# Modulation sums on TensorE, an input projection begun with the first half of them, and low parts made by VectorE

## What is computed

```python
mod = silu(c) @ w_ada + b_ada                       # c: (1, 2048), w_ada: (2048, 6 x 2048)
sh1, sc1, gt1, sh2, sc2, gt2 = split(mod, 6)
h = rms_norm(x, g_norm1) * (1 + sc1) + sh1
proj = h @ w_in                                     # 2048 x 3904: q, k, v (differential), latents cq, ckv, k_pe
a_out = differential_attention(...)                 # 8 heads
b_out = latent_attention(... w_q_b, w_kv_b ...)     # 8 heads
x = x + gt1 * (concat(a_out, b_out) @ w_out)
h2 = rms_norm(x, g_norm2) * (1 + sc2) + sh2
x = x + gt2 * ((silu(h2 @ w_gate) * (h2 @ w_up)) @ w_down)   # width 5632
```

## Time and profile before

| | |
|---|---|
| runs | 2667.58, 2671.43, 2675.92 us |
| profiled execution, span from first to last instruction | 2674.8 us |
| PE / PEld busy | 87% / 71% of the span |
| DVE / ACT / POOL busy | 40% / 37% / 78% |
| DMA, mean | 193 GB/s, 516.02 MB |

### The profile page before, as it was taken

The page is one execution under the profiler, slowest core; times in us unless marked ns, Lnnn a source line. Parts: engine busy times, 40 slices in busy tenths (PEclk is TensorE's granted clock), DMA queues, the critical chain, the costliest instruction groups (busy, mean ns, idle before and its releaser), DMA issues.

```text
span 2674.8 us, 29475 instructions
## 1 busy us (share of the span) xinstructions
PE 2319.1 (87%) x10218; PEld 1890.4 (71%) x10218; DVE 1066.6 (40%) x1189; ACT 1000.3 (37%) x1189; POOL 2095.1 (78%) x862
## 2 busy tenths in 40 slices
PE   0168984788899999999997966899999999999987
PEld 0157763476788888888886845787888888888765
DVE  4676458878611222111118399513111111111244
ACT  0023333433444444444443322344444444444433
POOL 0078965698888888888886875798888888888886
PEclk9879996789899999999998988999999999999998
DMA  7877744557666666666664633356666666666543
GB/s 254 261 258 246 253 158 137 185 189 266 236 200 206 207 205 205 205 205 208 205 204 142 190 117 102 126 190 191 190 189 190 192 189 189 190 192 189 173 151 133
DMA packets 241636, 516.02 MB, mean 193 GB/s; under 512 B 16429, under 2 KB 22274, under 8 KB 238882
## 3 DMA queue, kind: packets, MB, share of 16 engines
q1 hardware_dynamic: 239168, 512.55, 60.2%
q10 hardware_dynamic: 2402, 2.60, 0.6%
HBM read 510.90 MB, written 4.19 MB: 193 GB/s over the span
## 4 chain that ended last, share of the span: by engine, by line
PE 63%; DVE 8%; issue 3%; POOL 3%; DMA 3%; ACT 1%; DVEq 0%; SPq 0%; ACTq 0%
PE ps L1755 60%; DMA ada_raw<-in_w_ada 3%; POOL w_lo L816 2%; DVE ada_acc L1245 1%; DVE conv L928 1%; PE ps L1672 1%; POOL fm_lo L833 1%; PE ps L1770 1%; PE ps L1723 0%; DVE rstd L1177 0%; DVE y L1143 0%; DVE conv L1009 0%; PE ps L1897 0%; DVE x L1545 0%; DVE z L1267 0%
## 5 line engine op out<-in xcount | busy, mean ns | idle before, releaser
L816 POOL TENSOR_TENSOR w_lo<-raw,w_hi 128x1024 fp32r<-128x1024 f32 (+1 forms) x766 | 1921.9, 2517 | 464.7 <-ACT w_hi L574 464.0
L574 ACT ACTIVATE w_hi<-raw 128x1024 fp32r<-128x1024 f32 (+1 forms) x766 | 808.9, 1057 | 1389.1 <-PE ps L1755 1291.4
L1755 PE MATMUL ps<-w_hi,fm_hi 128*128 128x512 f32 (+1 forms) x2176 | 861.8, 396 | 83.5 <-POOL w_lo L816 59.9
L1755 PE MATMUL ps<-w_hi,fm_lo 128*128 128x512 f32 (+1 forms) x2176 | 851.9, 392 | 0.0
L1755 PE MATMUL ps<-w_lo,fm_hi 128*128 128x512 f32 (+1 forms) x2176 | 851.5, 391 | 0.0
L1755 PEld LDWEIGHTS ps<-w_hi,fm_hi 128*128 128x128 f32 x2176 | 413.2, 190 | 189.2 <-POOL w_lo L816 58.9
L1755 PEld LDWEIGHTS ps<-w_lo,fm_hi 128*128 128x128 f32 x2176 | 412.9, 190 | 86.7
L1755 PEld LDWEIGHTS ps<-w_hi,fm_lo 128*128 128x128 f32 x2176 | 413.5, 190 | 82.6
L1755 PE MATMUL ps<-w_hi,hid_hi 128*128 128x512 f32 x704 | 277.3, 394 | 2.5 <-issue 2.5
L1755 PE MATMUL ps<-w_lo,hid_hi 128*128 128x512 f32 x704 | 275.1, 391 | 0.0
L1755 PE MATMUL ps<-w_hi,hid_lo 128*128 128x512 f32 x704 | 274.9, 391 | 0.0
(11 more groups left out here) (281 smaller groups left out, 1801.0 us busy)
## 6 DMA issues: line engine op xcount, KB each, us to landing
raw<-in_w_gate SPq DMA_DIRECT2D x176, 512.0 KB, 3.7
raw<-in_w_up SPq DMA_DIRECT2D x176, 512.0 KB, 3.7
raw<-in_w_down SPq DMA_DIRECT2D x176, 512.0 KB, 3.7
ada_raw<-in_w_ada SPq DMA_DIRECT2D x160, 512.0 KB, 5.0
raw<-in_w_in SPq DMA_DIRECT2D x120, 512.0 KB, 3.7
raw<-in_w_out SPq DMA_DIRECT2D x64, 512.0 KB, 3.9
ada_wide<-in_w_ada SPq DMA_DIRECT2D x16, 1024.0 KB, 5.7
raw<-in_w_ple_gate SPq DMA_DIRECT2D x32, 512.0 KB, 3.7
```

The lines of the kernel that those rows point to most:

```text
L574: act.activation(w_hi[:, hi_slot, :, 0:width], raw[:, slot, :, 0:width], ACT.Copy).then_inc(hi_ready, 1)
L816: pool.tensor_tensor(w_lo[:, slot, :, 0:width], raw[:, slot, :, 0:width], w_hi[:, hi_slot, :, 0:width], ALU.subtract).then_inc(lo_ready, 1)
L1755: last = pe.matmul(banks[t][:, 0:width], a, b, start=kt == 0 and k == 0, stop=kt == kts - 1 and k == 2)
```

## The change

- w_ada for the first five vectors comes in 80 pieces of 128 rows by 2048 columns (1 MB) in five groups of 16: first half of sh1 and sc1, second half, the same of sh2 and sc2, then gt1. TensorE takes a piece as four fp32 matmuls of 32 columns of weights (c_act repeated 32 times) by 512 columns, each into its own 32 partitions of one PSUM bank (`ada`). A finished group is copied by ScalarE (`copy_rows`), turned by four transposes (`turn_columns`) and read by VectorE (`modulation`); for gt1 four matmuls spread the rows (`spread_gate`).
- The operand is turned and copied to `fm_t` before the modulation is known. in1 begins with the first half of the k-tiles of its first three units (pieces 0 to 11), with group 1's pieces between them; the second half follows. Groups 2 and 3 lie in in1 and q_b, group 4 in attention, one piece a step.
- VectorE makes the low parts of pieces 0 to 105 (`rest`), and the low parts of the operands up to out1 (`h1_lo`, `turned_lo`); GpSimd starts with the feed-forward.
- b_ada for gt1 is loaded after attention. `ada_acc` is only for gt2. A few PSUM banks change places.

```diff
-RAW, SPLIT, ADA = 6, 3, 4
+RAW, SPLIT = 6, 3
+ADA = 4
+ADA_GROUPS = ((0, 2, 0), (0, 2, 1), (3, 5, 0), (3, 5, 1), (2, 3, None))
+LO_DVE = FIRST["ffn1"]
+IN1_ORDER = (6, 7, 0, 1, 2, 3, 4, 5)
+IN1_HALVES = 3
@@ SyncE
+            def ada(n):
+                if n >= ADA:
+                    sp.wait_ge(ada_used, n - ADA + 1)
+                first, end, half = ADA_GROUPS[n // KT]
...
+            for n in range(10):
+                ada(n)
+            for n in range(RAW):
+                ada(10 + n)
+                weights(n)
+            for n in range(16, 22):
+                ada(n)
+            for i in range(12):
+                weights(i + RAW)
+                ada(22 + i)
+            for n in range(34, 38):
+                ada(n)
+            for i in range(12, FIRST["out1"]):
+                weights(i + RAW)
+                if i < FIRST["q_b"] and i % 4 == 3:
+                    ada(38 + (i - 15) // 2)
+                    ada(39 + (i - 15) // 2)
...
+            sp.wait_ge(ada_used, ADA_PIECES)
+            sp.dma_start(gate[:, :], ...)
@@ VectorE
+            def rest(p):
+                slot, width = p % RAW, in1_width(p) if p < FIRST["q_b"] else NW
+                dve.wait_ge(hi_ready, p + 1)
+                dve.tensor_tensor(w_lo[:, slot, :, 0:width], raw[:, slot, :, 0:width], w_hi[:, p % SPLIT, :, 0:width],
+                                  ALU.subtract).then_inc(lo_dve, 1)
...
+            for p in range(FIRST["out1"]):
+                rest(p)
+                if p == AHEAD - 1:
+                    modulation(0, shift1, ...)
+                    h1_operand(0)
+                if p == 11 + AHEAD:
+                    modulation(1, shift1, ...)
+                    h1_operand(1)
+                for r in range(8):
+                    if p == in1_end(r) + AHEAD - 1:
+                        in1_evacuate(r)
@@ TensorE
+            def ada(n):
...
+                pe.wait_ge(ada_landed[n % ADA], 16 * (n // ADA + 1))
+                for q in range(4):
+                    last = pe.matmul(ps[32 * q:32 * q + 32, ada_bank(group), :], c_wide[:, kt, :],
+                                     ada_raw[:, n % ADA, q * NW:(q + 1) * NW], start=kt == 0, stop=kt == KT - 1)
+                last.then_inc(ada_used, 1)
...
+            for p in range(4 * IN1_HALVES):
...
+                in1(p)
+                ada(KT + 2 + p)
+            ada(2 * KT - 2)
+            ada(2 * KT - 1)
+            turn_columns(1)
...
+            for p in range(4 * IN1_HALVES, FIRST["q_b"]):
...
+                in1(p)
+                if p % 4 == 3:
+                    ada(2 * KT + 2 + (p - 15) // 2)
+                    ada(2 * KT + 3 + (p - 15) // 2)
```

## The result

| | before | after |
|---|---|---|
| runs, median (lowest to highest), us | 2673.68 (2667.58 to 2676.66) | 2571.82 (2569.35 to 2574.93) |
| profiled execution's span, us | 2674.8 | 2570.1 |
| PE / PEld / DVE / ACT / POOL busy | 87 / 71 / 40 / 37 / 78% | 92 / 72 / 34 / 39 / 66% |

A forecast was written before the change was run, and what follows sets the result against it. PE was idle until its first product, then bound the input projection; DVE bound heads 0 to 7, later heads were mixed. Gains 40 + 8 + 14 + 11 + 10 = 83 off 2674.8, less 3.4: 2588 us, range 2560 to 2615.

The forecast's parts named there:

- Price of a piece: 1 MB w_ada piece on PE: 1.2 us, from 0.86 with four strips at once plus 0.34 for mode entry and exit.
- Start: Before in1's second half: DMA brings 45.9 MB at 320 GB/s by 143 us, operand ready at 149.
- DMA share above 0.9 from 10 to 150 us: Sign expected in the changed kernel's profile, during the loads up to in1's second half.
- Rest of in1: 52 pieces, 26 w_ada pieces at 1.2, DVE stalls of 6: 180 us, ending at 329.
- Heads 0 to 7: Attention, DVE-bound: w_ada sums and POOL's interference go, low parts come, net 9, gain 8 us (0 to 15).
- Heads 8 to 15: Attention on PE: eight steps of 5.7 and 8 for the last two, 54 against 68.6, gain 14 us (0 to 20).
- Output projection: No w_ada in DMA or on DVE: 91.7 against 102.4 us, gain 11.
- The term for spreading the gate: In the output projection: 4 x 0.86 = 3.4 us of PE.
- Tail: Output projection's last product to first gate product: 15 us instead of 24.6, gain 10.
- the first (strips in turn): w_ada strips run one after another, 3.44 us a piece: 2693 us; slower above about 2.97 per piece; chance 0.10.
- The second (DMA cannot hold 328 GB/s): In in1 DMA gives 290 GB/s, in1 ends 33 us later: 2621 us; chance 0.13.
- The third (DVE's low parts late): In in1 PE stands 25 us rather than 6, and a few in out1: 2611 us; chance 0.13.

The follow-up runs named there:

- experiment 7: Changed kernel with the 2 MB store of the relative bias rows moved behind the operand's second half, about 150 us: 2581.84 us, ratio 0.9650 to the kernel before.
- experiment 5: Changed kernel with GpSimd given two idle 128x1024 additions in each of the sixteen heads: 2592.26 us, ratio 0.9692 to the kernel before.
- experiments 1, 2: Changed kernel, from each group's second piece all four w_ada matmuls writing one strip: 2710.62 us; or strips 0, 1, 0, 1: 2601.41 us.
- (4): Changed kernel with in1 begun only when groups 0 and 1 are summed and both operand halves made: 2584.07 us, ratio 0.9658 to the kernel before.
- (3): Changed kernel with the low parts of pieces 0 to 105 made by GpSimd again: 2574.92 us, ratio 0.9631 to the kernel before.

## Why the prediction was right, and where its sizes were off

The mechanism came out as forecast: the strips overlap, in1 starts on half the modulation, and every stage that it named gained. The sizes were off, nearly all on the low side. Profile against profile the prediction missed 21.7 us of gain (104.7 against 83), and it looks closer, 16 us, by luck: I took off 3.4 us since the span stood over the median, where in every execution on record the time is 1.7 to 2.0 us over the span. The profiled execution of the kernel before was the longest of its four, then (2674.8 and some 1.8 make 2676.6), and that hides some 5 us of the miss. By its own steps:

- **Price of a piece: 1.2 taken, 0.93 measured** (1.0 alone). All four strips overlap: 3.49 in one strip, 1.78 in two, 0.93 in four, each time the number of strips. The chosen lower end of 0.86 was right; the entry into the strip mode was too dear. A piece alone takes 0.99 between starts (462.49 to 463.48), two take 1.85, so a second one behind a first costs 0.86 and a group of strips bears 0.13 besides, not 0.34. Here the Trainium skill, "TensorEngine Tiling (Array Packing)", Key Properties, says that a change of mode drains the engine; the trace does not show a drain as such, and all that it leaves for one is that 0.13 us. "TensorE: Matmul & The Clock Gate", Measured speedup vs the span model, has 2.38 times for three column tiles; here four give 6.98/1.85 = 3.8 times, so the measurement decides against carrying that efficiency over. In in1 the 26 pieces took 25.0 us of PE, not 31.
- **Start: 143 and 149 taken, 140.8 (start of the last piece) and 149.46 measured.** The number was right by a mean of two wrong parts. DMA did not run at a steady 320 GB/s: 398 from 20 to 40 us, before the store of experiment 7 was issued at 54, 272 and 180 from 60 to 100 beside it, 401 from 120 to 140 behind it, and 343 on average from 10 to 150. "DMA share above 0.9 from 10 to 150 us" holds for that average (0.96) and not from 60 to 100 (0.88 and 0.72). The first product came at 79.9, not 85.
- **Rest of in1: 180 taken, 170.8 measured.** Six of the nine are the pieces, 3.4 the low parts: PE waited 2.6 us for them, once, not 6. q_b and kv_b took 32.4, not 34.
- **Heads 0 to 7: 8 taken, 11.0 measured.** I counted POOL's interference on L1488 alone, 7 us. DVE's busy time fell by 15.7 (72.7 to 57.0) where I had a net of 9. L1488 gave its 7.1 us; besides, the scalings of attention had been stretched (L1490, 563 ns before, is 350 as L1497: 3.0 us) and the rotations of the latent heads (L1333, L1442, L1452: 3.5), and the w_ada sums were 7.6 us, not 5.4, for I had left out L1242. So POOL stood for some 13.6 us of DVE's time and the sums for 7.6, less some 5 for the low parts and a row maximum more; experiment 5 shows that a busy POOL does this to DVE, and no run splits the stage's 11.0 between the two. I was right that less than the whole comes through: DVE's idle time rose from 9.8 to 14.5 us, 9.5 of it waiting for the bias.
- **Heads 8 to 15: 14 taken, 19.1 measured.** The step is 5.6 us (424.10 to 463.48 is seven), as the 5.7 taken; the end was miscounted, eight steps and 8 us where there are seven and 9.3. Two things make the gain. PE's idle time fell from 14.7 us to 1.9, and its busy time from 53.0 to 46.8 us with 8 pieces (8.5 us) more in it, at a clock of 1.00 instead of 0.68. The longest wait before was 7.96 us for ACT's copy of a turned mix; ACT waited for a row maximum of DVE's, and DVE was at w_ada sums and at the reciprocal root for the norm of the differential heads, parts of it stretched by POOL. The 17 w_ada sums of this stage were 25.9 us of DVE. Windows of the kernel before, the whole stage first, and PE's row at the end of that wait:

```profile
485.80:553.58 67.78, 53.04 (x219) 36.95 (x217) 52.17 (x82) 27.12 (x86) 51.44 (x18) 0.68 0.53 173
...
509.70:518.69 8.99, 8.99 (x54) 6.33 (x53) 7.85 (x11) 5.21 (x19) 6.76 (x2) 1.00 0.54 179
...
527.00:536.00 9.00, 1.29 (x6) 1.29 (x7) 8.55 (x19) 2.23 (x7) 8.83 (x4) 0.69 0.38 126
536.00:545.00 9.00, 8.80 (x28) 5.80 (x27) 8.63 (x15) 1.74 (x6) 5.74 (x2) 0.50 0.79 243
```

```profile
534.71 2.07 PE L1897 MATMUL ps<-kv_mla,mixed_t 128*128 128x128 f32 x8 [7.96 <-ACT mixed_t L740]
```

The clock stood at 1.00 from 509.70 to 527 us, where PE hardly waited and took no w_ada piece, and at 0.50 behind the long wait. So a full clock does not need the pieces here, and that it is full now because the waits went is the likelier reading; it is argued, for no run leaves the pieces out. POOL's silence alone is worth 1.9 us here by experiment 5, where DVE has room without the sums.

- **Output projection: 11 taken, 13.9 measured.** It runs at PE's pace throughout, 88.2 us for 32 pieces and the gate. The term for spreading the gate was mis-sized, 1.1 us (501.09 to 502.16) for 3.4: the four matmuls take one partition each, in four different groups of 32, and overlapped too.

```profile
501.09 1.14 PE L1809 MATMUL ps<-gate_rows,ones 1*128 1x512 f32 x8
```

- **Tail: 10 taken, 9.0 measured.**

Of the rivals, the first (strips in turn) would have come true to within 18 us of its 2693 had the strips not overlapped. That is partly luck: its sum has a slip, for 12 x 5.9 after 80 is 151, and no turns make that 171, while the first product came at 98.1 instead of 80 and the second half at 184.8. The cost is no straight line in the price, 35 us per us from 0.93 to 1.78 and 64 from there to 3.49, so the break-even, an estimate between the last two, is 1.78 + (2673.7 - 2601.4)/64 = 2.9 us per piece, where I had 2.97. The second (DMA cannot hold 328 GB/s) failed on the average, 316 at a share of 0.90, without PE waiting for it; experiment 7 shows how near it was, for the 2 MB of the store in that stage cost 7 us. The third (DVE's low parts late) failed: PE waited 2.6 us for them.

What made the gain, then: w_ada's sums off DVE and POOL and onto strips of PE that cost 0.93 us a piece, which pays only since the strips overlap (experiments 1, 2); in1 begun early, 10 to 12 us of it (4); and in attention DVE without the sums and without POOL beside it, the two not split (5). No run puts the sums back on DVE; that their leaving shortened the start, in1 and attention is read from the waits of the two traces. Which engine makes the low parts of the weights is worth nothing that these runs can tell (3).

## What to carry to other kernels

A reduction that TensorE can do in narrow strips was cheap here only because neighbouring matmuls went to different strips: look at the distance of their starts before moving work there. When an engine waits for another's operation, follow that one's own wait: the longest wait for POOL's low parts was one for their data, and that one for a slot which a sum on DVE freed late. And find where a transfer with a poor rate costs least by trying: moved to a "later, calmer" place this one cost more.

## What was not expected of the hardware

- The 2.1 MB store (2 KB packets, q10) holds the DMA engines far longer than its size: in 60 to 100 us of the changed kernel it moved 1.91 MB at 31.0% of the engines' time, the loads 7.11 MB at 48.8%, so 2.4 times as much per byte. (Moved to 140 us it took 2.8 times as much per byte as the loads beside it, 1.58 MB at 21.7% and 10.72 MB at 52.9% from 140 to 200 us.) Why, no run shows.

```profile
q1 hardware_dynamic: 2117, 7.11, 48.8%
q10 hardware_dynamic: 933, 1.91, 31.0%
```

- Without it, loads of 1 MB ran 398 to 401 GB/s at a share of 1.04 (20 to 40 and 120 to 140 us), above the 355 that I had taken from the trace before as near the ceiling.
- POOL's additions slow DVE by kind of operation: in heads 0 to 7 of experiment 5 the mean of the scalings (L1505) and of one product (L1446) rose 1.7 times, that of another product (L1508) 1.2 times, 481 to 588 ns, and that of the reductions (L1485) not at all.
